# Gate and up weights of the experts in four transfers of 512 KB each

## The chip, the core and the metric

The kernel runs on one core of a Trainium2 chip. The core has five engines with queues of their own: PE (matrix products; PEld loads its weights), ACT (activations and copies), DVE and POOL (elementwise work), and SP, which here issues most of the transfers. Sixteen DMA engines move data between HBM and the core's on-chip memory (SBUF). A transfer issued on SP is spread over all sixteen and adds 16 to a semaphore when the whole of it has landed. The metric is the time of one execution on the device, in microseconds.

## The reference

One inference step of a two-layer encoder for 512 prompt rows and 32 sample rows of width 1024. Each layer has an attention mixer and then a mixture of 16 experts, of which each row uses two. All is float32. The part that the change touches is this:

```python
def _moe(h, w_router, b_router, w_gate, w_up, w_down):
    ...
    gates = jnp.sum(jax.nn.one_hot(idx, N_EXPERTS, dtype=jnp.float32) * w[..., None], axis=1)
    a = jax.nn.silu(jnp.einsum('nd,edf->nef', t, w_gate)) * jnp.einsum('nd,edf->nef', t, w_up)
    a = a * gates[:, :, None].astype(a.dtype)
    return jnp.einsum('nef,efd->nd', a, w_down).reshape(B, T, D)
```

Gate and up weights are 1024 x 512 for each expert, down weights 512 x 1024: 2 MB each.

## The kernel before

A layer runs in phases: attention, output projection with norm, routing, experts (`moe_*`), combine. Routing sorts the chosen rows by expert into items of up to 128 rows for one expert; the trace shows 17 items in each layer. An item needs 6 MB of weights (gate, up, down), a gather of its rows (`moe_in` to `m_x`), and a scatter of its results to `moe_out`.

Products are made from split operands. Each weight slab of 2 MB lands in `ring` (`m_low`), ACT writes a rounded copy of it (`split_high`, L2010, into `hT`, `work` or `arena` for gate, up and down), and DVE or POOL subtracts that copy from the slab in place (`split_low`, L2017, and POOL's `split`, L2493). PE then runs three products for each block of 128 weight rows (L590, L591, L592). Splitting goes by quarters of a slab: ACT does 0, 1, 2, 3, DVE subtracts 0, 2 and 3, POOL subtracts 1.

There is one slab buffer each for gate, up and down, so the gate slab of item n+1 is loaded once PE has finished gate of item n. `moe_sync` on SP does this in a loop, `turn`: wait for gate, issue the two halves of the next gate slab; wait for up, issue up; wait for down of the item before, issue down. A half is 1 MB, in each partition one run of 8 KB. ACT waits for the semaphore of half 0 ahead of quarter 0 and for that of half 1 ahead of quarter 2.

Each engine's order is written out by hand and is strict. In one turn PE does gate(n), turns the rows of n+1 (L2303), up(n), down(n-1), turns the activations of n (L2334). ACT does: activations' high part (L2391), split up 2 and 3, silu (L2387), split down 0 to 3, split gate(n+1) 0 and 1, evict the rows of n+1 (`rows_high`, L2381), split gate(n+1) 2 and 3, results of n-1 (L2399), split up(n+1) 0 and 1. DVE does: L2458, up 2 and 3, down 0, 2 and 3, gate(n+1) 0, rows' low part (L2447), the product of silu and up (L2454), gate(n+1) 2 and 3, up(n+1) 0. POOL does: down 1, the gather of the rows of n+2, gate(n+1) 1, the scatter of n-1, up(n+1) 1. So the turning of item n's activations on PE stands behind ACT's split of the next item's gate quarters 0 and 1, through L2381, L2447 and L2454.

Of the kernel before, what the change touches and what calls it, by code (L numbers as in the profile page):

```python
# [75 lines left out]
def encoder_step(nc, a, out, rope_dram):  # L76
    ctx = ExitStack()
    with ctx:
# [3 lines left out]
        def sems(prefix, *names):  # L82
            return {n: ctx.enter_context(nc.semaphore(f"{prefix}_{n}")) for n in names}
# [10 lines left out]
        def r32(ap):  # L94

            return bass.AP(tensor=rounded[ap.tensor.name], offset=ap.offset, ap=ap.ap)

        def f32(ap):  # L100

            return r32(ap).bitcast(F32)
# [260 lines left out]
        def mix_load(sp, l):  # L363

            mod_load(sp, l, 0, mod1[:, 0], "mix")
            mod_load(sp, l, 1, mod1[:, 1], "mix")
            norm_load(sp, l)
# [249 lines left out]
        def fuse_load(sp, l, b):  # L617

            g_b = NB * l + b
            if b >= 1:  # L620
                sp.wait_ge(FU["lo"], 4 * g_b)
                sp.wait_ge(FU["smp"], g_b)
            if l == 1:
                w = a["w_in_odd"][0][:, 0:QKV].rearrange("(k p) (s c) -> p k s c", p=P, s=3)
                c0 = P * b
            else:
                w = a["w_in_even"][0][:, 3 * CB * (b // N_DIFF):3 * CB * (b // N_DIFF + 1)].rearrange("(k p) (s c) -> p k s c", p=P, s=3)
                c0 = P * (b % N_DIFF)
            for h in range(2):
                dst = fu_raw[:, 4 * BW * h:4 * BW * (h + 1)].rearrange("p (k s c) -> p k s c", k=4, s=3)  # L630
                for k in range(4):
                    sp.dma_start(dst[:, k, :, :], w[:, 4 * h + k, :, c0:c0 + P]).then_inc(FU[f"raw{h}"], 16)
# [1322 lines left out]
        def out_pool(pool, l):  # L1955
            s, o = NORM, 2 * l + 1
            for j in OUT_POOL:
# [8 lines left out]

        MO = sems("mo", "wg0", "wg1", "wu0", "wu1", "wd0", "wd1", "wl0", "wl1", "hi_g", "hi_u", "hi_d", "lo_g", "lo_u", "lo_d",
                  "lop_g", "lop_u", "lop_d", "x", "tx", "xh", "xl", "g", "sg", "u", "a", "at", "ah", "al", "d", "ev", "y", "now_tok", "now_out")  # L1970
        m_x = arena[:, 0:1024]
        m_xh = arena[:, 1024:2048].rearrange("p (k c) -> p k c", k=KD)
# [6 lines left out]
        SLAB = KD * CB  # L1979
        m_low = {"g": ring[:, 0, :], "u": ring[:, 1, :], "d": ring[:, 2, :]}  # L1980
        m_high = {"g": hT_flat[:, 0:SLAB], "u": work[:, 0:SLAB], "d": arena[:, 10240:10240 + SLAB]}

        def slab_of(c, last_down):

            return "g" if last_down else c

        def piece(v, q):
            return v[:, SLAB // 4 * q:SLAB // 4 * (q + 1)]

        def item_no(eng, which):  # L1990
            i = {"first": 0, "last": 1, "end": 2, "last-1": 3}[which]
            return eng.value_load(n_items[0:1, i:i + 1], min_val=(0, 8, 9, 7)[i], max_val=2 * MAX_ITEMS)

        def first_item(eng, l):
            return 0 if l == 0 else item_no(eng, "first")
# [5 lines left out]
        def split_high(act, c, n, *pieces, last_down=None):  # L2001

            v = slab_of(c, last_down is not None)
            for q in pieces:
                if q in (0, 2):
                    if last_down is not None:
                        act.wait_ge(MO[f"wl{q // 2}"], 16 * last_down + 16)
                    else:
                        act.wait_ge(MO[f"w{c}{q // 2}"], 16 * n if c == "d" else 16 * n + 16)
                act.activation(r32(piece(m_high[v], q)), piece(m_low[v], q), ACT.Copy).then_inc(MO[f"hi_{c}"], 1)  # L2010

        def split_low(dve, c, n, *pieces, last_down=False):

            v = slab_of(c, last_down)
            for q in pieces:
                dve.wait_ge(MO[f"hi_{c}"], 4 * n + q + 1)
                dve.tensor_tensor(r32(piece(m_low[v], q)), piece(m_low[v], q), f32(piece(m_high[v], q)),  # L2017
                                  ALU.subtract).then_inc(MO[f"lo_{c}"], 1)

# [42 lines left out]
        def route_act(act, l):  # L2062
            s = RT
            act.preload_act_table_set("natural_log_exp_and_others")
            act.wait_ge(s["logits"], l + 1)
            act.activation(e_rows[:, 0:SEQ], bank[6][0:NE, :], ACT.Exp, scale=-1.0)
            act.activation(e_rows[:, SEQ:TOK], bank[7][0:NE, 0:DEC], ACT.Exp, scale=-1.0).then_inc(s["e"], 1)

            first = layer_first(act, l)
            split_high(act, "g", first, 0, 1, 2, 3)  # L2070
            split_high(act, "u", first, 0, 1)
            phase_end("act", act)
# [23 lines left out]
        def item_rows_in(pool, n, i):  # L2096

            pool.tensor_copy(now_tok[:, :], slot_tok[:, bass.ds(i, 1)]).then_inc(MO["now_tok"], 1)
            pool.wait_ge(MO["now_tok"], n + 1)
# [132 lines left out]
        def moe_sync(sp, l):  # L2232
            s = MO
            slabs = {"g": (a["w_gate"][l], KD), "u": (a["w_up"][l], KD), "d": (a["w_down"][l], KE)}

            def load(c, e, last_down=False):
                w, k = slabs[c]
                w = w[bass.ds(e, 1), :, :].rearrange("a (p k) c -> p (a k) c", k=k)
                for h in range(2):
                    sp.dma_start(m_low[slab_of(c, last_down)][:, SLAB // 2 * h:SLAB // 2 * (h + 1)].rearrange("p (k c) -> p k c", k=k // 2),  # L2240
                                 w[:, k // 2 * h:k // 2 * (h + 1), :]).then_inc(s[f"wl{h}" if last_down else f"w{c}{h}"], 16)


            sp.wait_ge(OUT["mm"], 10 * (l + 1))
            for c in "gud":
                load(c, 0)
            o = NORM_NO[f"norm_ffn{l}"]
            sp.wait_ge(NORM["shifted"], 3 * o + 3)
            sp.wait_ge(NORM["shift_v"], 2 * o + 2)
            sp.dma_start(moe_in[0:SEQ, :].rearrange("(t p) d -> p t d", p=P), h_rows[:, 0:NT, :]).then_inc(RT["h"], 16)  # L2250
            sp.dma_start(moe_in[SEQ:TOK, :], h_rows[0:DEC, NT, :]).then_inc(RT["h"], 16)
            sp.wait_ge(g["phase"], PH[f"route{l}"])
            first, last, end = first_item(sp, l), item_no(sp, "last"), item_no(sp, "end")

            def expert(n):
                i = nc.s_assert_within(n - first, 0, MAX_ITEMS - 1, skip_runtime_bounds_check_because="n is an item of this layer")
                return sp.value_load(item_expert[0:1, bass.ds(i, 1)], min_val=0, max_val=NE - 1)

            def turn(n, down):

                e = expert(n + 1)
                sp.wait_ge(s["g"], n + 1)
                load("g", e)
                sp.wait_ge(s["u"], n + 1)
                load("u", e)
                if down:
                    e = expert(n)
                    sp.wait_ge(s["d"], n)
                    load("d", e)

            turn(first, False)
            with sp.Fori(first + 1, last) as n:
                turn(n, True)
            e = expert(last)
            sp.wait_ge(s["g"], last + 1)
            load("d", e, last_down=True)
            if l == 0:
                fuse_load(sp, 1, 0)
            sp.wait_ge(s["d"], last)
            if l == 0:  # L2280
                mix_load(sp, 1)
            else:
                sp.dma_start(nf, a["norm_final"].partition_broadcast(P)).then_inc(AD["mix"], 16)
            sp.wait_ge(s["y"], 16 * end)
            for h in range(2):
                sp.sem_inc(s[f"wd{h}"], 16)
            for c in range(2):
                sp.dma_start(c_y[NT][c][0:DEC, :], moe_out[TOK * c + SEQ:TOK * (c + 1), :]).then_inc(CO[f"y{NT}"], 16)
            for t in range(NT):
                sp.dma_start(arena[:, c_at[t]:c_at[t] + 2 * D].rearrange("p (c d) -> p c d", c=2),  # L2290
                             moe_out.rearrange("(c n) d -> n c d", c=2)[P * t:P * (t + 1), :, :]).then_inc(CO[f"y{t}"], 32)
# [75 lines left out]
        def moe_act(act, l):  # L2367
# [7 lines left out]
            def split(c, n, *pieces):  # L2375
                split_high(act, c, n, *pieces)
# [319 lines left out]
```

## Time and profile before

| | us |
|---|---|
| median of 3 runs | 1675.86 |
| lowest, highest run | 1672.92, 1680.34 |
| the profiled execution | 1677.58 |
| its span, first to last instruction | 1675.8 |

The profile is of one execution. Its span leaves out 1.8 us around the instructions. Busy shares over the span are PE 85%, DVE 61%, ACT 52%, POOL 29%; these are means over stages with different limits. The two expert stages lie at about 500 to 845 us and 1327 to 1641 us. The mean granted TensorE clock is 0.919.

### The profile page before, as it was taken

How to read it: one execution, taken by the hardware profiler on the slowest of the kernel's cores; microseconds unless marked ns; L12 is line 12 of the kernel's file. 1: busy time of each engine (PE TensorE's matmuls, PEld its weight loads, DVE VectorE, ACT ScalarE, POOL GpSimd, SP SyncE). 2: the span in 40 equal slices, each digit the busy share in tenths (PEclk: the TensorE clock that was granted, in tenths of full speed). 3: DMA queues.
4: the chain of work that ended last, by engine and by line, in shares of the span. 5: the costliest groups of instructions: out<-in, count | busy, mean ns of one | idle time of the engine just before them, and what ended most of it. 6: DMA issues, size and time to landing. Idle time of an engine off the chain costs nothing.

```text
span 1675.8 us, 26415 instructions
## 1 busy us (share of the span) xinstructions
PE 1429.6 (85%) x9739; PEld 1146.4 (68%) x9739; DVE 1017.7 (61%) x1423; ACT 864.3 (52%) x1540; POOL 489.4 (29%) x372
## 2 busy tenths in 40 slices
PE   3799999988939999999927899999697499999981
PEld 2488877756727777887726788788476377878770
DVE  1555543235356989888856444443453577889975
ACT  2243445453125777887733344433422168878872
POOL 1301111110114656666511000000010156667650
PEclk7699999999958999999967999999799599999995
DMA  8356543242146989999951345432523189999974
GB/s 274 99 180 204 189 156 109 71 165 76 39 168 218 350 336 362 360 380 368 370 208 51 103 126 155 146 115 71 178 63 152 69 324 366 369 361 369 368 295 170
DMA packets 148234, 357.51 MB, mean 213 GB/s; under 512 B 18594, under 2 KB 80802, under 8 KB 122034
## 3 DMA queue, kind: packets, MB, share of 16 engines
q1 hardware_dynamic: 135796, 331.93, 55.0%
q0 software_dynamic: 12352, 24.40, 3.9%
q8 instruction: 58, 0.95, 0.2%
q14 instruction: 28, 0.23, 0.0%
HBM read 340.56 MB, written 33.54 MB: 223 GB/s over the span
## 4 chain that ended last, share of the span: by engine, by line
PE 64%; DMA 11%; DVE 10%; ACT 6%; issue 6%; SPq 1%; DVEq 1%; POOLq 0%; ACTq 0%; PEldq 0%; POOL 0%; PEld 0%
PE bank L590 15%; PE bank L591 14%; PE bank L592 14%; DMA ring<-in_w_gate 5%; PE bank L314 3%; DVE ring_r L2017 2%; DMA mod_rows<-ada_row 2%; PE bank L1513 2%; PE bank L1551 2%; PE bank L740 1%; ACT work_r L2010 1%; PE bank L1528 1%; PE bank L675 1%; DMA arena<-in_b_ada 1%; PE bank L2334 1%
## 5 line engine op out<-in xcount | busy, mean ns | idle before, releaser
L591 PE MATMUL bank<-ring_r,arena_r 128*128 128x512 f32 x816 | 322.4, 395 | 0.0
L590 PE MATMUL bank<-ring_r,hT_r 128*128 128x384 f32 x512 | 191.8, 375 | 0.0
L2017 DVE TENSOR_TENSOR ring_r<-ring,work_r 128x1024 fp32r<-128x1024 f32 x102 | 171.6, 1709 | 33.1 <-ACT work_r L2010 33.0
L591 PEld LDWEIGHTS bank<-ring_r,arena_r 128*128 128x128 f32 x816 | 156.1, 191 | 30.9
L2017 DVE TENSOR_TENSOR ring_r<-ring,arena_r 128x1024 fp32r<-128x1024 f32 x96 | 155.4, 1653 | 33.6 <-ACT arena_r L2010 33.6
L591 PE MATMUL bank<-ring_r,hT_r 128*128 128x384 f32 x512 | 172.8, 338 | 0.0
L592 PE MATMUL bank<-ring_r,work_r 128*128 128x384 f32 x512 | 172.8, 337 | 0.0
L2010 ACT ACTIVATE hT_r<-ring 128x1024 fp32r<-128x1024 f32 x144 | 144.2, 1054 | 50.2 <-DMA ring<-in_w_gate 46.3
L2017 DVE TENSOR_TENSOR ring_r<-ring,hT_r 128x1024 fp32r<-128x1024 f32 x108 | 144.7, 1368 | 28.5 <-ACT hT_r L2010 27.2
L2010 ACT ACTIVATE arena_r<-ring 128x1024 fp32r<-128x1024 f32 x128 | 127.7, 1052 | 37.7 <-DMA ring<-in_w_down 37.6
L2010 ACT ACTIVATE work_r<-ring 128x1024 fp32r<-128x1024 f32 x136 | 136.6, 1058 | 13.9 <-DMA ring<-in_w_up 13.8
L1961 POOL TENSOR_TENSOR arena<-arena,bc 128x1024 f32<-128x1024 f32 (+1 forms) x6 | 14.3, 2386 | 403.7 <-DVE arena L1947 403.7
L590 PE MATMUL bank<-hT_r,arena_r 128*128 128x512 f32 x288 | 121.2, 421 | 9.6 <-DVE arena_r L2458 6.5
L592 PE MATMUL bank<-hT_r,arena_r 128*128 128x512 f32 x288 | 117.1, 407 | 0.0
L2493 POOL TENSOR_TENSOR ring_r<-ring,arena_r 128x1024 fp32r<-128x1024 f32 x32 | 91.2, 2849 | 83.2 <-ACT arena_r L2010 83.2
L590 PE MATMUL bank<-work_r,arena_r 128*128 128x512 f32 x272 | 109.2, 402 | 0.0
L2493 POOL TENSOR_TENSOR ring_r<-ring,hT_r 128x1024 fp32r<-128x1024 f32 x36 | 90.5, 2515 | 61.7 <-ACT hT_r L2010 48.2
L592 PE MATMUL bank<-work_r,arena_r 128*128 128x512 f32 x272 | 106.4, 391 | 0.0
L590 PE MATMUL bank<-arena_r 128*128 128x512 f32 x256 | 100.6, 393 | 4.3 <-DVE ring_r L2017 4.0
L590 PEld LDWEIGHTS bank<-ring_r,hT_r 128*128 128x128 f32 x512 | 96.8, 189 | 10.3 <-issue 8.3
L592 PE MATMUL bank<-arena_r 128*128 128x512 f32 x256 | 99.8, 390 | 0.0
L591 PEld LDWEIGHTS bank<-ring_r,hT_r 128*128 128x128 f32 x512 | 97.3, 190 | 1.1 <-issue 0.7
(354 smaller groups left out, 2951.7 us busy)
## 6 DMA issues: line engine op xcount, KB each, us to landing
ring<-in_w_gate SPq DMA_DIRECT2D x68, 1024.0 KB, 7.4
ring<-in_w_up SPq DMA_DIRECT2D x68, 1024.0 KB, 7.8
ring<-in_w_down SPq DMA_DIRECT2D x68, 1024.0 KB, 8.0
bc<-in_w_ada SPq DMA_DIRECT2D x40, 1024.0 KB, 7.3
bc<-in_w_in_even SPq DMA_DIRECT2D x64, 192.0 KB, 3.9
bc<-in_w_in_odd SPq DMA_DIRECT2D x64, 192.0 KB, 3.6
ring<-in_w_ada SPq DMA_DIRECT2D x4, 2048.0 KB, 12.5
arena<-moe_out SPq DMA_DIRECT2D x8, 1024.0 KB
```

What stands on the lines that cost most here:

```text
L314: ins = nc.tensor.matmul(acc[32 * q:32 * q + 32, 0:AW], silu_c[:, k, :], w[:, AW * q:AW * (q + 1)], start=first, stop=last)
L590: nc.tensor.matmul(acc, rows_hi, w_hi, start=first, stop=False)
L591: nc.tensor.matmul(acc, rows_hi, w_lo, start=False, stop=False)
L592: return nc.tensor.matmul(acc, rows_lo, w_hi, start=False, stop=last)
L675: last = nc.tensor.matmul(acc[DEC * q:DEC * (q + 1), 0:SW], sample_T[:, k, :], w[:, k, SW * q:SW * (q + 1)], start=k == 0, stop=k == KD - 1)
L740: last = nc.tensor.transpose(out_bank[0:np_, c:c + r], src, ident[0:r, 0:r])
L1513: nc.tensor.matmul(fx_bank(u, h)[0:r, 0:n], fx_qT[i % 2][half, cols(t)], fx_kT[i % 2][half, k0:k0 + n], start=True, stop=False)
L1528: last = nc.tensor.transpose(fx_bank(u, h)[0:kr, r * n:r * n + r], fx_p[u % 2][h][0:r, c:c + kr], ident[0:r, 0:r])
L1551: last = nc.tensor.matmul(bank[6][half, c0:c0 + r], v, fx_pt[h][0:kr, r * n:r * n + r], start=n == 0, stop=n == len(tiles) - 1)
L2010: act.activation(r32(piece(m_high[v], q)), piece(m_low[v], q), ACT.Copy).then_inc(MO[f"hi_{c}"], 1)
L2017: dve.tensor_tensor(r32(piece(m_low[v], q)), piece(m_low[v], q), f32(piece(m_high[v], q)), ALU.subtract).then_inc(MO[f"lo_{c}"], 1)
L2493: pool.tensor_tensor(r32(piece(m_low[v], 1)), piece(m_low[v], 1), f32(piece(m_high[v], 1)), ALU.subtract).then_inc(MO[f"lop_{c}"], 1)
```

## The change

Gate and up slabs are loaded in four transfers of 512 KB (one run of 4 KB in each partition) with a semaphore for each, and ACT waits for one transfer ahead of each quarter. Down slabs keep their two halves. No arithmetic is changed.

```diff
-        MO = sems("mo", "wg0", "wg1", "wu0", "wu1", "wd0", "wd1", "wl0", "wl1", "hi_g", "hi_u", "hi_d", "lo_g", "lo_u", "lo_d",
+        MO = sems("mo", *(f"w{c}{q}" for c in "gu" for q in range(4)), "wd0", "wd1", "wl0", "wl1", "hi_g", "hi_u", "hi_d", "lo_g", "lo_u", "lo_d",
...
             for q in pieces:
-                if q in (0, 2):
+                if c != "d":
+                    act.wait_ge(MO[f"w{c}{q}"], 16 * n + 16)
+                elif q in (0, 2):
                     if last_down is not None:
                         act.wait_ge(MO[f"wl{q // 2}"], 16 * last_down + 16)
                     else:
-                        act.wait_ge(MO[f"w{c}{q // 2}"], 16 * n if c == "d" else 16 * n + 16)
+                        act.wait_ge(MO[f"wd{q // 2}"], 16 * n)
...
-                for h in range(2):
-                    sp.dma_start(m_low[slab_of(c, last_down)][:, SLAB // 2 * h:SLAB // 2 * (h + 1)].rearrange("p (k c) -> p k c", k=k // 2),
-                                 w[:, k // 2 * h:k // 2 * (h + 1), :]).then_inc(s[f"wl{h}" if last_down else f"w{c}{h}"], 16)
+                parts = 2 if c == "d" else 4
+                for h in range(parts):
+                    sp.dma_start(m_low[slab_of(c, last_down)][:, SLAB // parts * h:SLAB // parts * (h + 1)].rearrange("p (k c) -> p k c", k=k // parts),
+                                 w[:, k // parts * h:k // parts * (h + 1), :]).then_inc(s[f"wl{h}" if last_down else f"w{c}{h}"], 16)
```

On SP, the loop's gate and up part stands like this before (`mo_g` and `mo_u` are counted up by PE at the end of a gate and an up product):

```order
106 L2240 ISA [waits mo_g]
107 L2240 DMA ring<-in_w_gate 128x2048
108 L2240 ISA
109 L2240 DMA ring<-in_w_gate 128x2048
110 L2240 DMA ring<-in_w_up 128x2048 [waits mo_u]
111 L2240 DMA ring<-in_w_up 128x2048
```

and like this after it:

```order
110 L2243 ISA [waits mo_g]
111 L2243 DMA ring<-in_w_gate 128x1024
112 L2243 ISA
113 L2243 DMA ring<-in_w_gate 128x1024
114 L2243 ISA
115 L2243 DMA ring<-in_w_gate 128x1024
116 L2243 ISA
117 L2243 DMA ring<-in_w_gate 128x1024
118 L2243 DMA ring<-in_w_up 128x1024 [waits mo_u]
119 L2243 DMA ring<-in_w_up 128x1024 x3
```

Two more issues stand ahead of the wait for up, and two more behind it. On ACT, the splits of the next gate slab stand like this before, around the eviction of the rows:

```order
353 L2010 ACTIVATE hT_r<-ring 128x1024 [waits mo_wg0]
354 L2010 ACTIVATE hT_r<-ring 128x1024
355 L2381 ACTIVATE arena_r<-bank 128x512 [waits mo_tx,mo_u]
356 L2381 ACTIVATE arena_r<-bank 128x512 [waits mo_tx]
357 L2010 ACTIVATE hT_r<-ring 128x1024 [waits mo_wg1]
358 L2010 ACTIVATE hT_r<-ring 128x1024
```

and like this after it:

```order
353 L2012 ACTIVATE hT_r<-ring 128x1024 [waits mo_wg0]
354 L2012 ACTIVATE hT_r<-ring 128x1024 [waits mo_wg1]
355 L2384 ACTIVATE arena_r<-bank 128x512 [waits mo_tx,mo_u]
356 L2384 ACTIVATE arena_r<-bank 128x512 [waits mo_tx]
357 L2012 ACTIVATE hT_r<-ring 128x1024 [waits mo_wg2]
358 L2012 ACTIVATE hT_r<-ring 128x1024 [waits mo_wg3]
```

The order of the work is the same; each quarter has its own wait.

## Rows read from the trace of the kernel before

**Rows 1.** The page: span, and busy tenths in 40 slices.
```profile
span 1675.8 us, 26415 instructions
...
PE   3799999988939999999927899999697499999981
...
DMA  8356543242146989999951345432523189999974
GB/s 274 99 180 204 189 156 109 71 165 76 39 168 218 350 336 362 360 380 368 370 208 51 103 126 155 146 115 71 178 63 152 69 324 366 369 361 369 368 295 170
```
**Rows 2.** Timeline of SP's queue, gate and up: start us, us, line, transfer, count.
```profile
626.07 0.86 SPq L2240 DMA_DIRECT2D ring<-in_w_gate  x2
632.29 0.81 SPq L2240 DMA_DIRECT2D ring<-in_w_up  x2
```
**Rows 3.** Windows: stretch, us, busy by engine, PEclk, DMA share, GB/s.
```profile
529.88:547.69 17.81, 17.81 (x87) 14.91 (x86) 15.65 (x13) 14.80 (x19) 11.61 (x7) 1.00 0.91 340
626.07:810.63 184.56, 181.64 (x839) 148.19 (x837) 162.38 (x130) 148.41 (x179) 121.59 (x71) 1.00 0.96 368
...
1374.30:1597.62 223.32, 219.16 (x1011) 178.33 (x1010) 192.48 (x157) 179.70 (x217) 145.15 (x85) 1.00 0.97 367
```
**Rows 4.** Issues with median us to landing: 529 to 531 us, then 626.07 to 810.63.
```profile
ring<-in_w_gate SPq DMA_DIRECT2D x2, 1024.0 KB, 6.3
...
ring<-in_w_gate SPq DMA_DIRECT2D x21, 1024.0 KB, 8.5
```
**Rows 5.** Chain of waits, item at 681.78; last, ACT's timeline there.
```profile
681.78 7.52 DMA ring<-in_w_gate
...
691.33 0.49 ACT arena_r L2381
...
689.32 2.01 ACT L2010 ACTIVATE hT_r<-ring 128x1024 fp32r<-128x1024 f32 x2 [0.77 <-DMA ring<-in_w_gate]
```
**Rows 6.** Page's group of ACT; then waits, 626.07 to 810.63 and 1374.30 to 1597.62.
```profile
L2010 ACT ACTIVATE hT_r<-ring 128x1024 fp32r<-128x1024 f32 x144 | 144.2, 1054 | 50.2 <-DMA ring<-in_w_gate 46.3
...
ACT hT_r L2010 <- DMA ring<-in_w_gate: 13.1, 10, 2.5
...
PEld bank L590 <- issue: 3.5, 9, 1.1
PEld bank L2334 <- issue: 3.4, 5, 1.2
...
ACT hT_r L2010 <- DMA ring<-in_w_gate: 16.5, 12, 2.8
...
PEld bank L2334 <- issue: 5.6, 8, 1.3
PEld bank L590 <- issue: 5.0, 13, 0.8
```
**Rows 7.** Windows of 8 KB loads, of 4 KB loads, and of 4 KB loads with stores.
```profile
1286.00:1290.00 4.00, 4.00 (x20) 2.89 (x18) 1.36 (x2) 0.00 (x0) 0.00 (x0) 0.50 1.01 426
868.00:872.00 4.00, 0.00 (x0) 0.00 (x0) 3.90 (x4) 0.00 (x0) 0.00 (x0) 0.50 1.00 412
1649.00:1653.00 4.00, 0.00 (x0) 0.00 (x0) 3.90 (x5) 1.43 (x3) 0.00 (x0) 0.50 1.02 409
```
**Rows 8.** First turn of layer 0: chain of waits, then ACT's timeline.
```profile
512.12 5.17 DMA ring<-in_w_gate
...
517.31 2.00 ACT L2010 ACTIVATE hT_r<-ring 128x1024 fp32r<-128x1024 f32 x2 [4.74 <-DMA ring<-in_w_gate]
```
**Rows 9.** Timeline of SP's queue ahead of the loop in layer 1.
```profile
1283.19 1.16 SPq L2240 DMA_DIRECT2D ring<-in_w_down  x2
1287.46 0.38 SPq L2250 DMA_DIRECT2D moe_in<-arena  x1
```
**Rows 10.** DVE's and POOL's timelines, gate quarters 0 and 1, two items.
```profile
690.42 1.22 DVE L2017 TENSOR_TENSOR ring_r<-ring,hT_r 128x1024 fp32r<-128x1024 f32 x1
...
556.16 3.43 DVE L2017 TENSOR_TENSOR ring_r<-ring,hT_r 128x1024 fp32r<-128x1024 f32 x1
...
556.06 2.45 POOL L2493 TENSOR_TENSOR ring_r<-ring,hT_r 128x1024 fp32r<-128x1024 f32 x1
```

## The prediction, made before the changed kernel ran

> **What bounds the kernel now.** I read the page first [rows 1]. The change touches only the two expert stages, slices 14 to 20 and 33 to 38 of the 40. There PE stands at 9 tenths, the DMA engines at 9, and 324 to 380 GB/s are moved. Two resources are close to full at once, so shares alone don't say which one sets the pace. The next view is the SP queue [rows 2]: one turn of the loop issues gate, up and down, and the distance between two gate issues is the time of one item. The windows view then measures items [rows 3]. An item early in each layer takes 17.8 us with a DMA share of 0.91; PE is busy for all of it. Ten later items of layer 0 take 184.56 us (18.46 each) and twelve of layer 1 take 223.32 us (18.61 each), at shares of 0.96 and 0.97. So 17.8 us is what PE needs, and 22 later items lose 407.88 - 22 x 17.8 = 16.3 us to something else.
>
> The landings say to what [rows 4]. A first gate half lands 5.17 us after its issue when nothing is queued ahead [rows 8]; the median of two early gate halves is 6.3 us and that of the 21 in the later items 8.5 us. Up follows gate after 6.2 us [rows 2], each brings 2 MB, and three slabs share 18 us, so the transfers stand in line behind each other. In one late item, at 681.78 us, the chain of waits shows how this reaches PE [rows 5]: gate half 0 lands after 7.52 us, ACT splits two quarters of it (1.054 us each on average [rows 6]), then evicts the next item's rows (L2381), DVE subtracts (L2447) and multiplies silu by up (L2454), and only then can PE turn the activations (L2334). ACT had stood idle for 0.77 us before that split. ACT meets gate waits of 13.1 and 16.5 us in the two stretches, 22 in number [rows 6], and PE's weight loads idle 3.4 + 5.6 us ahead of L2334 and 3.5 + 5.0 us ahead of L590.
>
> I read this as follows: PE holds the pace for the first items of a layer, the queue of transfers builds up behind it, and from about the seventh item of layer 0 and the third of layer 1 the transfers hold it. What speaks against this is that the mean share is 0.96, not 1. The row traffic (indirect gathers and scatters) need not be spread evenly over the engines, and a slab is complete only when its slowest engine has finished.
>
> **The change, part by part.** *Earlier first quarter.* At the rate of an undisturbed run of 8 KB packets, 426 GB/s at share 1.01, thus 422 [rows 7], half a slab (1.05 MB) takes 2.5 us and a quarter 1.25 us. Quarter 0 lands 1.25 us before half 0 did, quarter 1 when half 0 did. ACT does quarter 0 while quarter 1 arrives, so both are ready up to one split earlier, 1.05 us, but never by more than ACT had waited. In the item at 681.78 us that is 0.77 us of a path on which PE was waiting. For up the same holds, but its quarters 0 and 1 are split at the end of ACT's turn, more than an item's gate product ahead of their use, so I count nothing there. Cover: when ACT has not waited, the gain is zero.
>
> *Where that gain goes.* If the transfers hold the pace, PE finishing 0.8 us earlier only issues the next load into a fuller queue. The allowance of about 1 us is used up once per layer, then landings are late again by as much as stalls PE. So I count it at places, not at every item: the first turn of a layer, where ACT waits 4.74 us and the chain runs through that wait [rows 8], gives 1.05 us in each layer, 2.1 together; the later stretches give at most 1 us in each, of which I count half. Together -3 us, with -2.1 and -6 as ends (a deeper queue also evens out the engines).
>
> *Smaller packets.* A half slab reads 8 KB runs in each partition, a quarter 4 KB. In the trace 8 KB loads alone move 422 GB/s; the combine step's loads of result rows (moe_out, 1024 values each) move 4 KB runs at 412 GB/s and share 1.00 in one window and 409 at 1.02, thus 401, in another where stores mix in [rows 7]. Gate and up are 4.19 MB an item: 9.94 us at 422, 10.18 at 412, 10.46 at 401. So +0.24 to +0.52 us of DMA time an item. The clean window is nearer to this case; with two more transfers to complete for each slab I take 0.30. While PE holds the pace this is hidden in the 8% of idle DMA time. In the 22 later items and the last one of each layer, 24, it is on the path: +7.2 us, ends 24 x 0.24 = 5.8 and 24 x 0.52 = 12.5. Below zero I see no reason to go.
>
> *Issues.* Four more issues an item on SP, at 0.34 to 0.43 us each: 0.9 us for gate becomes 1.8, and the next thing queued behind, the up issue, comes 6.2 us after gate [rows 2]. Hidden. The fourth quarter is issued some 1.3 us after the first while its data are due 3.75 us after it. Before the loop, six issues become ten, ahead of the store of the routed rows; in layer 1 the sixth ends at 1284.35 and the store waits until 1287.46 [rows 9], so four issues at up to 0.6 us (2.4 us) fit in 3.1. The waits themselves ride on the ACTIVATEs. Nothing is queued behind them that was not behind the half's wait before. Nothing.
>
> The Trainium skill, page "DMA: Bandwidth & Descriptors", section "Measured", says to batch transfers to 1 MiB or more for 75% of the peak, and gives 2.0 us fixed plus the bytes at 436 GB/s: by its formula a lone 512 KB transfer would run at 164 GB/s and a lone 1 MB at 238. The trace has the fixed part too (5.17 us for a half that moves in 2.5), but it is not paid again by a transfer that stands in line: six loads issued within 3.3 us moved 426 GB/s [rows 7, 9]. This is why that rule gets only the one-percent rival below.
>
> **The sum.** +7.2 - 3 = +4.2 us. The profiled execution took 1677.58 us (span 1675.8), the median of the runs is 1675.86; against the first this gives 1681.8, against the median 1680. I forecast 1680. Own range of this case: from 5.8 - 6 to 12.5 - 2.1, thus 1675.7 to 1686.3. Its upper end lies past +0.5% (8.4 us, about what a measurement of this kernel can tell from no change).
>
> **The rivals.**
> *A wait removed, faster.* The transfers do not hold the pace, only their lateness does: share 0.96 leaves 4% idle. Then every saved microsecond on ACT comes back, the packets' cost is hidden, and items go towards 17.8 us. There are 16.3 us to take in the later items; the 22 gate waits can give 23 at most. Leaving some 5 us for stalls that come from late pieces at L590, -11.3 - 3 = -14: 1662. For it: ACT does wait on gate and PE on ACT. Against: landings are late at every issue there, also at up and down.
> *Crowded packets, slower.* In the later items the rate at full share is 368/0.96 = 383 GB/s, not 422: an 8 KB packet takes 342 ns of an engine instead of 311. If these 31 ns are paid per packet, not per byte, each engine has 32 more packets an item (4.19 MB in 4 KB packets over 16 engines is 64, in place of 32), and 32 x 31 ns + 0.30 = 1.29 us an item, 24 times 31 us, less 3: +28, 1704. It decides once the price per item exceeds 0.48 us ((8.4 + 3)/24). For it: the crowding is real. Against: no row shows it to go by packets.
> *A new collision, slower.* DVE's subtraction of gate quarter 0 takes 1.22 us when it starts before POOL's of quarter 1, and 3.43 us in the item at 547.69 us, where POOL started 0.1 us earlier [rows 10]. ACT now ends quarter 1 earlier, so POOL could win more often, at 2.2 us each time; in eight items +17.7 on top of the forecast, 1698. It decides from two items on (4.2 us past the forecast's own 4.2). Against: POOL has its indirect issue ahead of this and often starts late because of that.
> *It does not do what it says.* The slowest engine carries the rows' traffic and its quarter 0 is no earlier, the packets cost nothing: 1676.
> *Each transfer pays its fixed part.* 5.17 - 2.5 = 2.7 us for four more transfers an item: 10.8 us in each of some 33 items, 2032.
>
> **Chances.** Forecast 0.46, of which 0.08 lies beyond +0.5%. Faster rival 0.24. Crowded packets 0.10, collision 0.04. No effect 0.15. Fixed part 0.01. So faster by over 0.5%: 0.24; within: 0.38 + 0.15 = 0.53; slower: 0.08 + 0.10 + 0.04 + 0.01 = 0.23. For the range I leave out the slow ends (crowded packets, collision, fixed part: 0.15) and the bottom of the faster case, 1661 downwards: 1661 to 1692.
>
> **What the profile of the changed kernel would show.** Right: ACT's waits on gate fall from 46.3 us [rows 6] by about half, items of the early stretch stay at 17.8 us, later ones stand at 18.6 to 18.9 us with the DMA share at 0.97 or more and landings of the last gate quarter later than the second half's now; the first turns are 1 us shorter. If later items go below 18.2 us the faster rival holds, and I was wrong on who holds the pace. If they exceed 19 us with PE waiting, the packets are dearer than I took. If DVE's subtraction of gate shows more pieces near 3.4 us, it is the collision. If ACT's gate waits stay as they are, nothing landed earlier.

## The result, and the profile after

| | before | after |
|---|---|---|
| median of 14 runs each, us | 1680.17 | 1670.38 |
| lowest to highest | 1672.92 to 1690.46 | 1663.77 to 1685.95 |
| the profiled execution | 1677.58 | 1669.46 |
| its span | 1675.8 | 1667.7 |

The ratio of after to before is 0.9949, with a 95% interval of 0.9926 to 0.9972: 8.6 us faster, between 4.7 and 12.4. The forecast had been 4 us slower.

The page of after answers to [rows 1]. Its columns are the same, 40 equal slices.

```profile
span 1667.7 us, 26735 instructions
...
PE   3699999987937999999927899999788399999981
...
DMA  7356643242054999999961334532423289999984
GB/s 265 96 179 204 202 160 109 72 165 77 0 205 157 370 354 363 369 374 383 377 222 51 103 122 143 164 116 71 166 76 116 102 297 374 369 375 375 373 305 171
```

In the expert stages the rate is up a little. Slices 14 to 20 moved 336 to 380 GB/s before and move 354 to 383 now. The windows view, with the columns of [rows 3], takes the same two stretches of ten and twelve later items, and one early item:

```profile
533.96:551.75 17.79, 17.79 (x87) 14.89 (x86) 14.71 (x13) 14.80 (x19) 11.61 (x7) 1.00 0.88 306
626.33:808.89 182.56, 181.35 (x843) 149.06 (x842) 161.60 (x131) 150.01 (x181) 120.86 (x71) 1.00 1.00 372
...
1370.93:1589.89 218.96, 217.95 (x1011) 178.83 (x1010) 191.43 (x157) 180.44 (x217) 144.77 (x85) 1.00 1.00 373
```

Ten items went from 184.56 to 182.56 us, twelve from 223.32 to 218.96. The early item stays at 17.8 us, PE's own time. The DMA engines' mean share in the later stretches rose from 0.96 and 0.97 to 1.00. This is where the forecast said that nothing more could be had.

Bytes alone don't explain the rise of the share: in the ten items the core moved 67.91 MB before and 67.92 after. The queues' view of the two stretches gives this for the loads' queue (packets, MB, share of the 16 engines' time), before and after:

```profile
q1 hardware_dynamic: 8577, 62.41, 88.5%
...
q1 hardware_dynamic: 14334, 62.42, 91.8%
```

With the queue of the rows (7.8% and 7.9%) that is 96.3% of 184.56 us, thus 177.7, and 99.7% of 182.56, thus 182.0 us of DMA time for the same bytes. In the twelve items of layer 1 it is 215.9 and 218.1. So the smaller packets do cost DMA time, 6.4 us in 22 items or 0.29 us an item, and the items still became shorter.

ACT's waits, answering to [rows 6]: first the groups of the page, then the waits of the stretch 626.33 to 808.89 us.

```profile
L2012 ACT ACTIVATE hT_r<-ring 128x1024 fp32r<-128x1024 f32 x144 | 145.9, 1054 | 18.2 <-DMA ring<-in_w_gate 14.7
L2012 ACT ACTIVATE arena_r<-ring 128x1024 fp32r<-128x1024 f32 x128 | 128.2, 1053 | 53.1 <-DMA ring<-in_w_down 53.1
...
ACT hT_r L2012 <- DMA ring<-in_w_gate: 2.4, 6, 1.0
PEld bank L2337 <- issue: 2.7, 5, 1.0
PEld bank L590 <- issue: 1.7, 6, 0.8
```

ACT waits 14.7 us in all for gate, in place of 46.3, and in this stretch 2.4 in place of 13.1. PE's weight loads idle 2.7 + 1.7 us ahead of the turning and ahead of products (3.4 + 3.5 before). ACT's wait for down grew, from 37.6 to 53.1 us.

The first turn of layer 0, answering to [rows 8], on ACT's timeline:

```profile
520.46 1.06 ACT L2012 ACTIVATE hT_r<-ring 128x1024 fp32r<-128x1024 f32 x1 [2.91 <-DMA ring<-in_w_gate]
521.96 1.06 ACT L2012 ACTIVATE hT_r<-ring 128x1024 fp32r<-128x1024 f32 x1 [0.45 <-DMA ring<-in_w_gate]
```

Gate was issued at 517.10 us. ACT's wait is 2.91 us instead of 4.74, and it begins quarter 1 at 4.86 us after the issue.

**Where the time went.** The distance between gate issues in SP's timeline gives every item's time. There are 16 such distances in layer 0 and 14 in layer 1; with the loads ahead of the loop that makes 18 items and 16, not 17 in each as I wrote above. Their sum is 557.3 us before and 545.5 after, so 11.8 us come from the expert loops. The span fell by 8.1 only: the first expert load is issued at 461.65 us instead of 455.15, behind attention code that the change doesn't touch, and routing and the rest gave some back. The runs of one kernel spread over 17 to 22 us, so a few microseconds outside the loop say nothing here. Of the 11.8 us, 6.4 come from the two later stretches, 1.6 from the two first turns, and the other 3.8 from the early items of layer 0.

The 30 distances fall into two kinds. Most are between 16.9 and 19.3 us. A few are 20.3 us or more; I call them **long items**. Before had two (20.5 and 22.3, 42.8 us together), after has one (20.5). The others have a mean of 18.38 us before and 18.10 after. So the profile shows two effects: 28 or 29 regular items gained 0.28 us each, some 8 us, and one long item fewer, some 2 to 4 us. All three long items lie ahead of the later stretches (they begin at 547.69 and 585.99 us before, at 588.02 after), so the 6.4 us there are of the first kind alone. The item behind a long one took 17.8 us, PE's own time, in these two kernels and in all that follow; such items are among the others and lower their mean where long items are many. The experiments are about these two effects.

### The profile page after: what moved, and what is told of

Same layout as the page of the kernel before. It is cut to its first block, busy times and chain, and to the rows that moved or that the text cites. A ratio compares the mean times of both kernels' runs of the same rounds, so it can differ in the third digit from the quotient of the medians.

```text
span 1667.7 us, 26735 instructions
## 1 busy us (share of the span) xinstructions
PE 1425.0 (85%) x9731; PEld 1148.0 (69%) x9739; DVE 1014.5 (61%) x1423; ACT 866.4 (52%) x1540; POOL 489.8 (29%) x372
## 4 chain that ended last, share of the span: by engine, by line
PE 73%; DVE 9%; DMA 7%; ACT 4%; issue 4%; SPq 3%; DVEq 1%; POOLq 0%; PEldq 0%; POOL 0%; ACTq 0%; PEld 0%
PE bank L590 18%; PE bank L592 17%; PE bank L591 17%; DMA ring<-in_w_down 3%; PE bank L314 2%; DMA mod_rows<-ada_row 2%; PE bank L1513 2%; PE bank L2306 2%; PE bank L1551 2%; DVE ring_r L2019 1%; PE bank L740 1%; PE bank L1528 1%; PE bank L675 1%; PE bank L2337 1%; PE bank L585 1%
## 5 line engine op out<-in xcount | busy, mean ns | idle before, releaser
L2019 DVE TENSOR_TENSOR ring_r<-ring,work_r 128x1024 fp32r<-128x1024 f32 x102 | 183.8, 1826 | 16.3 <-ACT work_r L2012 16.0
L2019 DVE TENSOR_TENSOR ring_r<-ring,arena_r 128x1024 fp32r<-128x1024 f32 x96 | 141.1, 1498 | 45.2 <-ACT arena_r L2012 45.1
L2012 ACT ACTIVATE arena_r<-ring 128x1024 fp32r<-128x1024 f32 x128 | 128.2, 1053 | 53.1 <-DMA ring<-in_w_down 53.1
L2012 ACT ACTIVATE hT_r<-ring 128x1024 fp32r<-128x1024 f32 x144 | 145.9, 1054 | 18.2 <-DMA ring<-in_w_gate 14.7
L592 PE MATMUL bank<-arena_r 128*128 128x512 f32 x256 | 99.7, 389 | 0.0
```

The costliest lines, as they stand in the source:

```text
L592: return nc.tensor.matmul(acc, rows_lo, w_hi, start=False, stop=last)
```

## The experiments

Those kernels that load otherwise than before or the change share one generalisation of the changed kernel: a table `LOADS` gives, for each slab, the transfers in eighths of a slab, grouped by semaphore. ACT waits for a group ahead of the quarter at which it begins, and `l` is the last down slab of a layer.

```diff
-                parts = 2 if c == "d" else 4
-                for h in range(parts):
-                    sp.dma_start(...).then_inc(s[f"wl{h}" if last_down else f"w{c}{h}"], 16)
+                at = 0
+                for i, group in enumerate(LOADS["l" if last_down else c]):
+                    for part in group:
+                        sp.dma_start(...).then_inc(s[f"wl{i}" if last_down else f"w{c}{i}"], 16)
+                        at += part
```

The results of all, ordered by ratio. Ratio and interval are of many runs; the last three columns are of the one profiled execution (30 distances between gate issues).

| kernel | ratio to before | 95% interval | median us | long items | mean of the others | sum |
|---|---|---|---|---|---|---|
| down in quarters too | 1.0037 | 1.001 to 1.0065 | 1688.66 | 11 | 17.95 | 578.0 |
| gate only | 1.0018 | 0.9987 to 1.0049 | 1684.91 | 4 | 18.22 | 557.2 |
| before | 1 | | 1680 | 2 | 18.38 | 557.3 |
| before, order fixed | 0.9968 | 0.9947 to 0.9988 | 1673.48 | 0 | 18.39 | 551.8 |
| quarters, waits for halves | 0.996 | 0.9937 to 0.9984 | 1672.85 | 1 | 18.37 | 553.3 |
| the change | 0.9949 | 0.9926 to 0.9972 | 1670.38 | 1 | 18.10 | 545.5 |
| quarters, waits for halves, order fixed | 0.9949 | 0.9925 to 0.9973 | 1671.49 | 0 | 18.43 | 553.0 |
| eighths | 0.9937 | 0.9916 to 0.9958 | 1670.43 | 1 | 18.26 | 551.6 |
| up only, order fixed | 0.9936 | 0.991 to 0.9961 | 1668.12 | 0 | 18.31 | 549.3 |
| up only | 0.9935 | 0.9909 to 0.996 | 1671.01 | 2 | 18.28 | 553.0 |
| down too, order fixed | 0.9932 | 0.9908 to 0.9956 | 1668.19 | 0 | 18.31 | 549.3 |
| gate only, order fixed | 0.9921 | 0.9896 to 0.9945 | 1665.84 | 0 | 18.29 | 548.8 |
| the change, order fixed at gate and down | 0.9906 | 0.9875 to 0.9937 | 1664.1 | 0 | 18.31 | 549.3 |
| the change, order fixed | 0.9895 | 0.9866 to 0.9925 | 1664.88 | 0 | 18.24 | 547.3 |

The last kernel has only six runs. The quotient of their median and that of the runs of before beside them (1678.64) is 0.9918, not 0.9895; a gain that rests on it is given from both.

### Which slab, and is it the wait or the transfer's size?

```diff
 # gate only
+        LOADS = {"g": [[2], [2], [2], [2]], "u": [[4], [4]], "d": [[4], [4]], "l": [[4], [4]]}
 # up only
+        LOADS = {"g": [[4], [4]], "u": [[2], [2], [2], [2]], "d": [[4], [4]], "l": [[4], [4]]}
 # quarters, ACT waits for halves
+        LOADS = {"g": [[2, 2], [2, 2]], "u": [[2, 2], [2, 2]], "d": [[4], [4]], "l": [[4], [4]]}
 # down in quarters too
+        LOADS = {"g": [[2], [2], [2], [2]], "u": [[2], [2], [2], [2]], "d": [[2], [2], [2], [2]], "l": [[4], [4]]}
```

> Gate in four transfers of 512 KB with a wait each, up and down in two of 1 MB as before. Hand-off theory (the gate slab's late first quarter was holding ACT, and PE behind it, while the DMA engines still had 4% to spare): nearly the whole gain stays, 6 to 10 us below the kernel before, later items at 18.2 to 18.3 us, ACT's gate waits in all near 15 us. Throughput theory of the forecast (the transfers hold the pace, packets of 4 KB cost time): half of the packets' cost, so this is not better than the change, and the later items stay at 18.4 us or more. Luck theory (the change only met fewer collisions of DVE and POOL): within 3 us of the kernel before.

> Up in four transfers of 512 KB with a wait each, gate and down in two of 1 MB as before. Hand-off theory: gate's quarter 0 and 1 are as late as before, so 0 to 2 us gained or up to 3 lost, ACT's gate waits stay at 40 us or more. A theory that smaller transfers as such run better (they start sooner after the issue, whatever ACT waits for): half the gain of the change, 4 us. Throughput theory: 3 to 4 us slower.

> The transfers of the changed kernel (gate and up in four of 512 KB), but ACT waits for two of them ahead of quarters 0 and 2, as for the halves before: the transfers' size without the finer wait. Hand-off theory: most of the gain is gone; what is left is that the first two quarters land about 0.3 us sooner after the issue than a half did (4.84 us against 5.17 in the first turns), so 0 to 3 us below the kernel before. Sooner-start theory: 5 us or more below it. Throughput theory: 5 to 8 us above it.

> The changed kernel with down also in four transfers of 512 KB with a wait each (the last down slab of a layer stays in halves). Hand-off theory as it stands after the change: ACT's largest wait is now on down (53 us in all), but down's quarters stand ahead of gate's in ACT's order and the DMA engines are at a share of 1.00, so at most 3 us more are gained, and the packets' 0.12 to 0.26 us an item may take them back: 1666 to 1672 beside a changed kernel of 1670. If a slab's first quarter matters wherever ACT waits: 5 us or more beyond the change.

No theory had all four right. Gate only gave nothing (1.0018), up only gave as much as the whole change (0.9935), transfers in quarters without the finer wait gave 0.4% (6.7 us, what the sooner-start theory had said), and down in quarters, which I expected to be harmless, made the kernel slower than before (1.0037). The luck theory, which I had put last, described gate only best.

The profiles say why. In gate only ACT's waits on gate fell as expected, to 16.7 us, and its regular items are shorter (18.22 against 18.38, in part because four of them stand behind long ones), but there are four long items. In down too eleven items are long. The others have the lowest mean of all kernels, 17.95 us, but ten of these nineteen stand behind a long item and took 17.8. This is one long item with the one behind it as windows, then DVE and POOL in the long one:

```profile
663.29:685.59 22.30, 20.15 (x87) 15.94 (x86) 21.71 (x15) 15.06 (x19) 12.95 (x8) 0.92 0.91 336
685.59:703.41 17.82, 17.82 (x87) 14.92 (x86) 13.95 (x12) 14.88 (x19) 10.67 (x7) 1.00 0.92 315
...
671.91 3.44 DVE L2020 TENSOR_TENSOR ring_r<-ring,hT_r 128x1024 fp32r<-128x1024 f32 x1
...
671.80 2.46 POOL L2499 TENSOR_TENSOR ring_r<-ring,hT_r 128x1024 fp32r<-128x1024 f32 x1
```

DVE comes late, from its last down quarters. POOL starts gate quarter 1 at 671.80, 0.1 us before DVE could start quarter 0. DVE's subtraction takes 3.44 us where one alone takes 1.2, and everything behind it on DVE (L2453, the product, and so PE's turning) moves by some 2.2 us. It is the event of [rows 10], and it was my third rival. The timelines of all seven kernels without a fixed order hold 22 long items, and each of them has this event: POOL is first by about 0.1 us and DVE's subtraction takes 3.43 or 3.44 us. In no other item of these kernels does it take more than 2 us.

The lateness has a row too. In the first long item of the kernel before, as in all 22, DVE's three down quarters took 5.7 us in a row instead of 3.6:

```profile
550.53 5.71 DVE L2017 TENSOR_TENSOR ring_r<-ring,arena_r 128x1024 fp32r<-128x1024 f32 x3
...
547.69:568.20 20.51, 18.53 (x87) 14.79 (x86) 20.51 (x15) 14.79 (x19) 12.69 (x8) 1.00 0.90 354
```

DVE had lost 2.1 us to POOL's down quarter 1 one step earlier, and so it lost the start at gate. That loss at down stands in 10 items before (2 of them long), 8 with gate only (4), 9 with up only (2), 7 with quarters and half waits (1), 16 with down too (11), but only 2 in the change (1) and 1 in eighths (1). In down too ACT waits only 13.7 us for down in all, so down's splits come in one block.

The window rows show a second cost. The item at 547.69 has its granted clock at 1.00 and took 20.5 us, the one at 663.29 has 0.92 and took 22.3. In both PE waits 1.7 us for L2454's product (L2460 in down too). In the second the clock is then at 0.50, which is 1.2 GHz of 2.4, from about 678.85 to 682.20 us, and PE's products start 0.43 us apart instead of 0.23. Of the 22 long items 13 took 20.3 to 20.7 us at 1.00, and 9 took 22.0 to 22.3 us at 0.92. So a collision costs an item some 2.2 us, and in 9 of 22 cases 1.8 us more by PE's clock. What decides which of the two follows was not tried.

What a finer wait gives with one hand it can take with the other, depending on which of two engines arrives first.

### Fixing the order of the two engines

If this is the cause, an order between the two subtractions should remove the long items from every kernel.

```diff
                 pool.wait_ge(MO[f"hi_{c}"], 4 * n + 2)
+                if c == "g":
+                    pool.wait_ge(MO["lo_g"], 3 * n + 1)
                 settle(pool)
```

> The kernel before, with one more wait on POOL: gate quarter 1 is subtracted only after DVE has subtracted gate quarter 0, so that the order of the two is fixed. Collision theory (where POOL starts first, DVE's subtraction takes 3.4 us instead of 1.2 and the item 20.3 us or more instead of 17.8 to 19; such long items, 2 in the profile of before, 1 after, 4 in the gate-only kernel, 11 with down too, explain the order of those kernels): no item over 19.5 us, 4 to 10 us faster than before. If the long items come from something else and the late DVE subtraction is only a sign of it: as many of them as before, time within 3 us of it or slower, since POOL's part is now later.

> The changed kernel with the same one wait more on POOL. Collision theory: no item over 19.5 us, 2 to 6 us faster than the changed kernel, thus 1664 to 1668 beside 1680 for the kernel before. The difference to the kernel before with this wait would be the pure gain of the finer hand-off, which regular items put at 0.28 us each (18.38 before, 18.10 after), 8 us in all. Otherwise: as the changed kernel, 1670.

> Gate, up and down all in four transfers (which was 0.4% slower than before), with the one wait more on POOL. Collision theory: its eleven long items (237 us) shrink to about 18 us each, so 25 to 40 us faster than without the wait: 1650 to 1663, the best kernel of all. Otherwise it stays at 1680 or more.

In all three no item is over 19.5 us. In the kernel before with this wait, DVE has its 1.2 us and POOL waits 0.89 us for it:

```profile
652.21 1.23 DVE L2017 TENSOR_TENSOR ring_r<-ring,hT_r 128x1024 fp32r<-128x1024 f32 x1 [0.40 <-ACT hT_r L2010]
...
653.63 2.39 POOL L2495 TENSOR_TENSOR ring_r<-ring,hT_r 128x1024 fp32r<-128x1024 f32 x1 [0.89 <-DVE ring_r L2017]
```

That kernel is 0.3% faster than before (expected 4 to 10 us; 5.4 by the ratio). With the change's transfers the same wait gives 0.9895 (1665 us, as expected), and with down too 0.9932: from 1.0037, some 17 us. I had expected 25 to 40 us there and the best kernel of all. Its long items are gone, and so are the short ones behind them: the mean of the others went from 17.95 to 18.31 us, while ordinary later items stand at 18.4 to 18.5 us in both profiles. The sum of the distances fell by 28.7 us, some 2.6 for each long item. In its ordinary item DVE is busy for 17.95 of 18.48 us:

```profile
639.93:658.41 18.48, 18.08 (x87) 14.86 (x86) 17.95 (x14) 15.15 (x19) 11.89 (x8) 1.00 0.98 357
```

Part of that is time in which DVE's operations stretch beside POOL's: 25 of the 28 items with a down product have the full loss of 2.1 us at down. The DMA share is 0.98 there, so both are near full, and which of them sets 18.4 us was not tried.

### The transfers' parts with the order fixed

With collisions out of the way the first four experiments can be read again. Each has its own `LOADS` line from above and the wait on `lo_g`; the last has it at down as well (`if c in "gd": pool.wait_ge(MO[f"lo_{c}"], 3 * n + 1)`).

> Gate in four transfers with a wait each, up and down in halves, and POOL's subtraction of gate quarter 1 fixed behind DVE's of quarter 0. Without this order gate only gave nothing (ratio 1.0018, four long items). Theory of two terms (a finer hand-off of gate gives 0.16 us in each regular item, collisions take it back): with the order fixed no long items, and 3 to 7 us below the kernel before with the same order (1673), thus 1666 to 1670. If it stays at 1673 or above, gate's finer hand-off gives nothing and its gain in the change is up's.

> Up in four transfers with a wait each, gate and down in halves, the order of POOL and DVE at gate fixed. Up only gave 0.65% without it. Two terms: up's share of the hand-off is the smaller (0.10 us an item), so 1 to 4 us below the kernel before with the same order: 1669 to 1672, and no faster than up only without the order by more than 3 us (1668 to 1671). If up is the source of the gain, it is at 1666 or below and equal to the changed kernel with the order (1665).

> Gate and up in four transfers, but ACT waits for two at a time, and the order of POOL and DVE at gate fixed: the transfers' size without the finer wait, and without collisions. If the finer wait makes the gain: as the kernel before with the order, 1672 to 1675. If the smaller transfers do (they start sooner after the issue: a first quarter lands 3.3 us after it, a half 5.2): as the changed kernel with the order, 1665.

> The changed kernel with POOL's quarter 1 fixed behind DVE's quarter 0 both at gate and at down. If collisions at down cost path time of their own (13 subtractions of down still take over 2 us with gate's order alone), 1 to 4 us more are gained: 1661 to 1664. If only the one at gate stands on PE's path, it is within 2 us of the changed kernel with gate's order (1665), or slower, since POOL's gather of rows now starts later.

The medians were 1665.84, 1668.12, 1671.49 and 1664.1 us. They lie at or within 1 us of what the theory of two terms, the finer wait and the gate collision alone had said. Against the kernel before with the order fixed (0.9968), quarter transfers without the finer wait give 0.2% (0.9949; the intervals overlap, so it may be nothing). Quarters with the finer wait give 0.3% at up (0.9936; the intervals overlap a little), 0.5% at gate (0.9921) and 0.5 to 0.7% at both (0.9918 or 0.9895). Only the last two are clear of the kernel that they start from, and they are not clear of each other. Between quarters without and with the finer wait at both (0.9949 and 0.9895) the intervals only touch; the medians are 1671.49 and 1664.88 us. Both intervals of gate only are telling: 0.9987 to 1.0049 without the order, 0.9896 to 0.9945 with it. Beside the kernel that it starts from, the same edit is worth nothing in the one case and 8 us in the other. For up only the order changes nothing (0.9935, 0.9936), though its profile without the order held two long items. Fixing down's order too gives nothing beyond gate's (0.9906): once the order at gate is fixed, the losses at down that are left cost nothing that these runs can tell.

### Do the DMA engines hold the pace?

```diff
+        LOADS = {"g": [[1, 1], [1, 1], [1, 1], [1, 1]], "u": [[1, 1], [1, 1], [1, 1], [1, 1]], "d": [[4], [4]], "l": [[4], [4]]}
```

> The changed kernel with gate and up in eight transfers of 256 KB (runs of 2 KB), two on one semaphore, ACT waiting once per quarter as in the changed kernel: the packets' cost doubled again, the hand-off unchanged. If the DMA engines hold the pace at their share of 1.00: about 0.6 to 0.9 us more for each later item, 14 to 22 us above the changed kernel. If they do not: within 5 us of it, or moved only by the number of long items.

The packets of gate and up are half as long once more, and the kernel is no slower than the change: 0.9937 (0.9916 to 0.9958) beside 0.9949. Its windows in the later stretches (the first is of 172 us inside layer 0, the second of twelve items):

```profile
631.00:803.00 172.00, 169.64 (x778) 138.79 (x777) 147.72 (x120) 139.55 (x167) 109.17 (x65) 0.99 1.00 366
1374.00:1594.03 220.03, 218.06 (x1011) 178.82 (x1010) 189.95 (x157) 181.36 (x218) 144.02 (x85) 1.00 1.01 374
```

The share stands at 1.00 and 1.01, the rate at 366 and 374 GB/s beside 372 and 373 in the changed kernel, and twelve items take 220.0 us beside 219.0. The 14 to 22 us that I had expected of a throughput limit are not there. But the sum behind them charged twice the packets' cost, and the queues show less: 100.7% of 220.03 us are 221.6 us of DMA time for twelve items beside 218.1, some 0.2 to 0.3 us an item. A limit would have cost 5 to 7 us by that, and the profiled sum is 6.1 us longer (551.6 against 545.5), 1.5 of it because its long item is of the longer kind. So this run rules out packets that cost 0.6 us an item or more. It does not show that the transfers hold nothing back in the changed kernel, whose share is 1.00.

## Why the prediction was wrong

**The step that failed** is the third paragraph of the first part: that from the seventh item of layer 0 and the third of layer 1 the transfers hold the pace. I took late landings and a share of 0.96 as a full queue. The landings were late, but the remaining idle share was room: the same bytes need 0.29 us more of DMA time an item after the change, and the 22 later items, without a long one in either profile, take 401.5 us instead of 407.9. Had the transfers held the pace, they could only have become longer. Whether the transfers hold the pace after the change, at share 1.00, is open. The argument against my reading stood there in one sentence (the share is not 1), and I explained it away by an uneven spread that no row showed.

**The packets' cost**, +7.2 us, came out of that step. Its size was right, 0.29 us of DMA time an item against the 0.30 that I took from the rates of [rows 7]; it was not on the path.

**The gain of the earlier first quarter**, -3 us, was mis-sized for the same reason. The mechanism was the one described in [rows 5]: ACT's wait on gate, then L2381, L2447, L2454, then PE. I allowed it once per layer and half a microsecond beyond, where the regular items gained 0.28 us each in the two profiles. With collisions fixed, transfers and waits together are worth 9 us by the medians (1673.48 and 1664.88) and 12 by the ratios (0.9968 and 0.9895). The two profiled executions of that pair show less, 4.5 us in the loops (551.8 and 547.3), all of it in layer 0. In the first turns, where I counted 1.05 us each, the distance fell from 17.8 to 16.9 and from 17.7 to 17.0 us.

**Up at nothing** was wrong as well. Up only, with the order fixed, is at 0.9936 against 0.9968, some 5 us, though the intervals overlap a little, and without the order at 0.9935 (0.9909 to 0.996). I had named the distance between ACT's split and its use as the cover, but DVE and POOL stand behind that split; through which of them the gain reaches PE was not traced.

**The issues at nothing** was right: gate's four issues take 1.90 us and up's stand 6.2 us behind.

**The rivals.** The faster one (1662, chance 0.24) had the right mechanism, with 14 us against the measured 8.6: the later items gave 6.4 of the 16.3 us that were there, and ended at 18.25 us instead of near 17.8. The collision (chance 0.04, slower) was real, but it does not act in one direction. In the profiled executions it was there twice before the change and once after, four times with gate only and eleven times with down too. It is the main reason why neighbouring edits differ by 1%: the same wait on POOL moved gate only from 1.0018 to 0.9921 and down too from 1.0037 to 0.9932. Crowded packets, fixed part and no effect fell: none of these fits 0.9937 for eighths and ACT's 14.7 us.

**The signs I had named**: ACT's gate waits fell by two thirds, not half; the DMA share rose to 1.00, as written for my case; but the later items stood at 18.26 and 18.25 us, under the 18.6 to 18.9 of my case and just over the 18.2 that I had put for the faster rival. The sign of the share alone would have confirmed the wrong theory. The sign of the collision, DVE's subtraction near 3.4 us, was there once in gate's quarter 0 after the change and twice before.

**What stays open.** Why the change itself has few collisions while gate only and down too have many is shown in part: the collision at gate comes only where DVE has lost 2.1 us at down, in 2 items of the change and 16 of down too. What sets that loss is argued: down landed late in the change (ACT waited 53.1 us for it), which spaces out DVE's down quarters, and early in down too (13.7 us). Before (37.6 us, two long items), gate only (39.8, four) and up only (38.1, two) lie between without an order of their own. Up only's runs are also better than its profiled execution (sum 553.0) suggests. No experiment set the landing of down by itself.

## What to carry to other kernels

A resource at a mean share of 0.96 whose transfers land late is not yet a limit. Late landings and a limit look alike in a profile. What told them apart here was the time that the resource needs for the same bytes, beside the time that the loop takes: the first rose and the second fell. Adding overhead to the resource, as eighths did, tells only as much as the overhead measures. Where two engines take turns at work that stretches when it overlaps, an early input can make the wrong one start first. Before judging a finer hand-off, look for items of the loop that are much longer than the others, and fix the order with a wait: that was worth 0.3% alone and 1% for gate only, and with the change it gave the best kernels here (1664 to 1665 us, 0.9895 to 0.992 of before).

## What the runs showed of the hardware

A transfer's time ahead of its data is not quite a constant. With nothing queued ahead, the first transfer of gate's first turn landed after 5.17 us for 1 MB in 8 KB packets [rows 8], and the issues view has these times for the first transfer of 512 KB in 4 KB packets (the changed kernel) and of 256 KB in 2 KB packets (eighths):

```profile
ring<-in_w_gate SPq DMA_DIRECT2D x1, 512.0 KB, 3.3
...
ring<-in_w_gate SPq DMA_DIRECT2D x1, 256.0 KB, 2.7
```

Less the bytes' own time at 422 GB/s (2.5, 1.25 and 0.62 us), 2.7, 2.1 and 2.1 us are left. In the first two turns of each layer, in all the kernels here, the landing times are 5.0 to 5.6 us, 3.3 to 3.8 and 2.7 to 2.9, so between 512 and 256 KB nothing differs, and 1 MB has a few tenths more. I had expected 2.7 for all, and so a first quarter after 3.9 us; it came after 3.3. In eighths ACT waits for two transfers of 256 KB and began 3.57 us after the issue, no sooner than in the changed kernel (3.36). The Trainium skill, page "DMA: Bandwidth & Descriptors", section "Anatomy of one DMA — SWDGE (gpsimd) path", gives about 2.0 us fixed, independent of the size, for the path through GpSimd. On SP's queue these loads come near it at 512 and 256 KB and have 0.7 us more at 1 MB. (The prediction names the section "Measured" for this figure and not its path; it stands in the section named here.)

A subtraction on DVE that starts 0.1 us behind one of POOL's waits for nearly the whole of the other: 1.2 us became 3.44 beside a POOL operation of 2.46, and 3.43 or 3.44 in all 22 cases.

A wait of 1.7 us on PE, with PE at 1.00 of its clock before, can be followed by 0.50: in 9 of the 22 long items, at 1.8 us each.
